# Splitting the positions around the second norm of the first block in a two-block kernel on one core

## The reference

```
merged = sigmoid(g_att) * y_att + sigmoid(g_conv) * y_conv
x = x + rms_norm(merged @ w_out, norm_mix_post)      # w_out 1024 x 1024
h = rms_norm(x, norm_ffn_pre)
u = causal_dwconv(h @ w_up, conv_ffn_w)              # w_up 1024 x 5632, three taps along the positions
a, g = split(u)
f = (gelu(g) * a) @ w_down                           # w_down 2816 x 1024
x = x + rms_norm(f, norm_ffn_post)
```

## Time and profile before

| | |
|---|---|
| median of 3 runs | 902.0 us (901.87 to 902.0) |
| the profiled execution, span from first to last instruction | 900.7 us |
| TensorE matmuls busy | 888.3 us |
| VectorE, ScalarE, GpSimd busy | 571.0, 496.2, 136.0 us |
| granted TensorE clock | 1.00 (2.4 GHz) over the span |
| share of TensorE in the chain that ended last | 83% |

### The profile page before, as it was taken

The page is one execution under the profiler, slowest core; times in us unless marked ns, Lnnn a source line. Parts: engine busy times, 40 slices in busy tenths (PEclk is TensorE's granted clock), DMA queues, the critical chain, the costliest instruction groups (busy, mean ns, idle before and its releaser), DMA issues.

```text
span 900.7 us, 15634 instructions
## 1 busy us (share of the span) xinstructions
PE 888.3 (99%) x6451; PEld 821.5 (91%) x6451; DVE 571.0 (63%) x824; ACT 496.2 (55%) x771; POOL 136.0 (15%) x151
## 2 busy tenths in 40 slices
PE   8999999999999999999999999999999999999998
PEld 8999999889999988788899988999999899998886
DVE  4556554878888746666767797765467655554542
ACT  5576864556656634566776764423454565554330
POOL 6011101611111100133443110000100011110000
PEclk9999999999999999999999999999999999999999
DMA  7843364665665566346544546542345656656560
GB/s 279 275 155 118 95 227 150 232 207 181 199 199 179 188 210 214 131 169 242 182 141 144 160 133 177 155 135 77 115 140 191 187 168 202 193 187 204 181 200 23
DMA packets 132594, 156.33 MB, mean 174 GB/s; under 512 B 9353, under 2 KB 106028, under 8 KB 132268
## 3 DMA queue, kind: packets, MB, share of 16 engines
q1 hardware_dynamic: 125844, 151.78, 51.9%
q10 hardware_dynamic: 6680, 3.56, 1.3%
HBM read 153.08 MB, written 2.24 MB: 172 GB/s over the span
## 4 chain that ended last, share of the span: by engine, by line
PE 83%; DVE 8%; DMA 3%; ACT 3%; issue 1%; POOL 1%; SPq 0%; ACTq 0%; POOLq 0%
PE ps L1979 72%; PE ps L1934 4%; PE ps L2010 3%; DVE wl L828 2%; PE ps L1931 2%; PE ps L2235 2%; DVE gv L862 1%; DVE gkq L862 1%; DMA U<-blocks 1%; DMA raw<-in_w_in 1%; DMA blocks<-last 1%; DVE mt L1267 1%; DMA Yc<-inverses 1%; ACT wh L1426 1%; DMA inverses<-Y 0%
## 5 line engine op out<-in xcount | busy, mean ns | idle before, releaser
L828 DVE TENSOR_TENSOR wl<-raw,wh 128x1024 fp32r<-128x1024 f32 (+1 forms) x275 | 326.4, 1205 | 190.0 <-ACT wh L1426 189.9
L1979 PE MATMUL ps<-xh,wh 128*128 128x256 f32 x1280 | 357.3, 282 | 0.7 <-ACT xh L1474 0.7
L1979 PE MATMUL ps<-xh,wl 128*128 128x256 f32 x1280 | 350.6, 277 | 0.0
L1426 ACT ACTIVATE wh<-raw 128x1024 fp32r<-128x1024 f32 (+1 forms) x292 | 286.6, 1024 | 115.4 <-PE ps L1979 93.0
L1979 PE MATMUL ps<-xl,wh 128*128 128x256 f32 x1280 | 348.3, 277 | 0.0
L1979 PEld LDWEIGHTS ps<-xh,wh 128*128 128x128 f32 x1280 | 238.9, 188 | 4.5 <-issue 1.4
L1979 PEld LDWEIGHTS ps<-xh,wl 128*128 128x128 f32 x1280 | 238.8, 188 | 0.0
L1979 PEld LDWEIGHTS ps<-xl,wh 128*128 128x128 f32 x1280 | 238.0, 188 | 0.3
L669 POOL TENSOR_TENSOR wl<-raw,wh 128x1024 fp32r<-128x1024 f32 (+1 forms) x17 | 44.2, 2600 | 81.6 <-ACT wh L1426 81.3
L1979 PE MATMUL ps<-wh,f2L 128*128 128x512 f32 x128 | 49.8, 389 | 0.0
L1979 PE MATMUL ps<-wl,f2H 128*128 128x512 f32 x128 | 49.8, 389 | 0.0
(11 more groups left out here) (334 smaller groups left out, 1363.8 us busy)
## 6 DMA issues: line engine op xcount, KB each, us to landing
raw<-in_w_in SPq DMA_DIRECT2D x55, 1024.0 KB, 5.1
raw<-in_w_up SPq DMA_DIRECT2D x38, 1024.0 KB, 5.2
raw<-in_w_down SPq DMA_DIRECT2D x26, 1024.0 KB, 5.0
raw<-in_w_out SPq DMA_DIRECT2D x8, 1024.0 KB, 5.1
raw<-in_w_proj_fox SPq DMA_DIRECT2D x4, 1024.0 KB, 5.1
raw<-in_w_proj_gdn SPq DMA_DIRECT2D x4, 1024.0 KB, 5.1
raw<-in_w_conv_branch SPq DMA_DIRECT2D x4, 512.0 KB, 3.4
raw<-in_w_att_branch SPq DMA_DIRECT2D x4, 512.0 KB, 3.3
```

The costliest lines, as they stand in the source:

```text
L828: e.tensor_tensor(L, R, H.bitcast(F32), ALU.subtract).then_inc(lo.sem)
L1426: e.activation(tile_of(WH, u)[:, k:kc, :], tile_of(RAW, u)[:, k:kc, :], ACT.Copy).then_inc(hi.sem)
L1979: k = e.matmul(o, l, r, start=opens, stop=done and n == ends[c], skip_group_check=True)
```

## The change

The last two output projection units (30, 31) are run by `part` first for positions 0 to 127 and then for 128 to 255, and so are the first two up units (32, 33) by a new `first_up`, which takes them with the activations stationary (as mode A does, 256 columns), into banks 7 and 3. The second norm is done for one half at a time by the functions that the second block's input already used, now with an index n. What units 32 and 33 give has positions on partitions; ScalarE copies it to XS (`keep_first_up`) and TensorE turns it back into the banks the convolution reads (`first_up_turn`). Their convolutions start in unit 34. The warm-up matmuls ahead of this norm and in it are gone. Unit 33 takes the fourth buffer pair. The low second half of unit 33, which VectorE made beside unit 31's `post`, is made with the first half, and both of unit 33's high halves stand ahead of ScalarE's `post` of unit 31. GpSimd does for each half both factors. The sync engine loads the gains of the norm (now applied from a row GN instead of a column) ahead of unit 33's weights, and spreads the loads that waited for the residual. The small weights are converted behind unit 40 instead of 32.

The diff, cut:

```diff
-WARM = (12, 4, 12)
+WARM = 12
-LATE_LO = frozenset([33])
...
+        AHEAD1, BEHIND1 = range(U_UP - 2, U_UP), range(U_UP, U_UP + 2)
+        AHEAD2, BEHIND2 = range(U_FQ - 3, U_FQ), range(U_FQ, U_FQ + 3)
+        SPARE = (BEHIND1[1], BEHIND2[0])
+        home, behind = {}, {}
+        for u in range(NU):
+            home[u] = NW if u in SPARE else (u - sum(s < u for s in SPARE)) % NW
+            behind[u] = max((v for v in range(u) if home[v] == home[u]), default=None)
...
+        FIRST_UP = (PS[7], PS[3])
... (sync)
-            for u in range(NRAW, U_UP + 3):
+            for u in range(NRAW, U_UP + 1):
+                weights(u)
+            e.wait_ge(*ymd("m", 3))
+            e.dma_start(GN[:], norm_ffn_pre[0].partition_broadcast(P)).then_inc(ld_gn, 16)
+            for u in range(U_UP + 1, U_UP + 5):
                 weights(u)
             e.wait_ge(*px("x", 1))
             e.dma_start(GP[:], norm_ffn_post[0].partition_broadcast(P)).then_inc(ld_gp, 16)
+            e.wait_ge(*nsc("up", 3))
             e.dma_start(GN[:], norm_mix_g_2[0].partition_broadcast(P)).then_inc(ld_gn, 16)
+            for u in range(U_UP + 5, U_UP + 10):
+                weights(u)
+            e.wait_ge(*ended(BEHIND1[1]))
             e.dma_start(gsw[:, :, 0:16], ...
-            for u in range(U_UP + 3, NU):
+            for u in range(U_UP + 10, NU):
... (GpSimd)
-            rstd(prs, 0, ss[:, 2:3], pred("sum", 0))
-            rstd(prs, 1, ss[:, 3:4], pred("sum", 1))
+            low(BEHIND1[0])
             for a in range(2):
+                rstd(prs, a, ss[:, 2 + a:3 + a], pred("sum", a))
                 e.wait_ge(*px("x", a))
                 rstd(nrs, a, ss[:, a:a + 1], nsq("sq", 2 + a))
... (VectorE, behind unit 29 and its post)
+            part(BEHIND1[0])
+            part()
+            low(BEHIND1[1], 0)
+            low(BEHIND1[1], 1)
+            post(0, AHEAD1[1], 1, 0)
+            x2_scaled(1, 0)
+            post(0, AHEAD1[1], 1, 1, ends=False)
+            x2_low(1, 0, 0)
+            post_ends(0, 1)
+            x2_low(1, 0, 1)
+            low(U_UP + 2, 0)
+            x2_scaled(1, 1)
+            low(U_UP + 2, 1)
+            x2_low(1, 1, 0)
+            x2_low(1, 1, 1)
+            part()
+            part(U_UP + 3)
...
+            for v in range(2, FC1):
+                unit(U_UP + v, 4 if v == 2 else None, first_up)
... (ScalarE, behind unit 29 and its post)
+            part(BEHIND1[0])
+            part(BEHIND1[1])
+            post(0, AHEAD1[1], 1, 0)
+            e.wait_ge(*px("x", 0))
+            squares(0)
+            high(U_UP + 2, 0)
+            post(0, AHEAD1[1], 1, 1)
+            x2_high(1, 0, 0)
+            x2_high(1, 0, 1)
+            e.wait_ge(*px("x", 1))
+            squares(1)
+            high(U_UP + 2, 1)
+            x2_high(1, 1, 0)
+            x2_high(1, 1, 1)
...
+            keep_first_up(0)
+            part()
+            part(U_UP + 3)
+            keep_first_up(1)
...
+            def first_up():
+                e.wait_ge(*upt("t"))
+                conv_begins(0)
+                conv_begins(1)
... (TensorE)
+            def first_up(u, a, at=None, begins=None):
+                H, L = tile_of(WH, u), tile_of(WL, u)
+                o = FIRST_UP[a][:, 256 * (u - U_UP):256 * (u - U_UP) + 256]
+                order = [(q, j) for q in range(8) for j in (0, 2)] + [(q, 1) for q in range(8)]
...
+                    k = e.matmul(o, (XH, XL, XH)[j][:, q, a * P:(a + 1) * P], (H, H, L)[j][:, q, :], start=n == 0, stop=n == 23,
...
+            def first_up_turn(a):
+                e.wait_ge(*upk("k", a))
+                for j in range(2):
...
+                    for c in range(2):
+                        k = turn(main_ps(U_UP + j)[:, c * 256 + a * P:c * 256 + (a + 1) * P],
+                                 XS[:, a, j * 256 + c * P:j * 256 + (c + 1) * P])
+                if a:
+                    k.then_inc(upt.sem)
+                    settle(7)
...
-            warm(WARM[0])
-            norm(1)
-            for v in range(FC1):
-                unit(U_UP + v, XH, XL, **(x_of(1) if v == 0 else {}))
-                if v == 0:
-                    settle(7)
+            for a in range(2):
+                for u in AHEAD1:
+                    part(u, a, m1H, m1L, lambda a, q: ymh("hi", q // 2), lambda a, q: ymd("lo", q // 2))
+            x2_turn(1, 0, 0)
+            x2_turn(1, 0, 1)
+            first_up(BEHIND1[0], 0)
+            first_up(BEHIND1[1], 0, at=3, begins=lambda: x2_turn(1, 1, 0))
+            x2_turn(1, 1, 1)
+            first_up(BEHIND1[0], 1)
+            first_up(BEHIND1[1], 1, at=2, begins=lambda: first_up_turn(0))
+            for v in range(2, FC1):
+                unit(U_UP + v, XH, XL, at=2 if v == 2 else None, begins=lambda: first_up_turn(1))
```

More of the change, by code:

```diff
@@ L1271, in vector, with first_convs @@
                     y_att_low(i)
-            def first_post(i):
-                if i:
-                    low(U_UP + 1, 1)
-                post(0, U_WO + 2 * i + 1, i, 0)
-            for i in range(2):
-                u = U_WO + 2 * i + 1
-                unit(u - 1)
-                unit(u, 5, lambda i=i: first_post(i))
-                post(0, u, i, 1)
-            scaled(1, 0)
-            scaled(1, 1)
-            norm(1, CG["ffn"])
-            soon.add(small_weights_low())
-            for v in range(FC1):
-                unit(U_UP + v)
+            u = U_WO + 1
+            unit(u - 1)
+            unit(u, 5, lambda: post(0, u, 0, 0))
+            post(0, u, 0, 1)
+            part(BEHIND1[0])
[15 more added lines that the diff above has]
+            part(U_UP + 3)
+            def first_convs():
+                yield from up_conv(0, 1)
+                yield from up_conv(1, 1)
+            def first_up():
+                soon.add(first_convs())
+            for v in range(2, FC1):
+                unit(U_UP + v, 4 if v == 2 else None, first_up)
                 soon.add(up_conv(v))
+                if v == 8:
+                    soon.add(small_weights_low())
+                if v == 2:
+                    soon.add(f_low(0))
                 if v % 2:
@@ L1421, in high @@
                     e.wait_ge(raw[s], 16 * (u // NRAW + 1))
-                    if u >= NW and u != U_FQ:
-                        e.wait_ge(*ended(u - NW - int(u in FIRST_X2)))
+                    if behind[u] is not None:
+                        e.wait_ge(*ended(behind[u]))
+                    elif u == SPARE[0]:
+                        e.wait_ge(*ymd("lo", 3))
                 elif u == 0:
@@ L1782, in scalar, with keep_first_up, conv_begins @@
                     y_att_high(i)
-            for i in range(2):
-                u = U_WO + 2 * i + 1
-                unit(u - 1)
-                unit(u, 5, lambda u=u, i=i: post(0, u, i, 0))
-                post(0, u, i, 1)
-            for a in range(2):
-                e.wait_ge(*px("x", a))
-                squares(a)
-            norm(1, CG["ffn"])
-            soon.add(small_weights_high())
-            for v in range(FC1):
-                unit(U_UP + v)
+            u = U_WO + 1
+            unit(u - 1)
+            unit(u, 5, lambda: post(0, u, 0, 0))
+            post(0, u, 0, 1)
+            part(BEHIND1[0])
[12 more added lines that the diff above has]
+            x2_high(1, 1, 1)
+            def keep_first_up(a):
+                end_of(BEHIND1[1], a)
+                copy(XS[:, a, 0:512], FIRST_UP[a][:]).then_inc(upk.sem)
+            keep_first_up(0)
+            part()
+            part(U_UP + 3)
+            keep_first_up(1)
+            def conv_begins(v):
                 i = v // 2
                 dst, cbase = (ya, yg)[v % 2][i % 2], (CG["cfa"], CG["cfg"])[v % 2] + 2 * FC1 + 2 * i
-                end_of(U_UP + v)
                 if i >= 2:
@@ L1804, in scalar, with first_up @@
                     soon.add(up_gelu(i))
+            def first_up():
+                e.wait_ge(*upt("t"))
+                conv_begins(0)
+                conv_begins(1)
+            for v in range(2, FC1):
+                unit(U_UP + v, 4 if v == 2 else None, first_up)
+                end_of(U_UP + v)
+                conv_begins(v)
+                if v == 8:
+                    soon.add(small_weights_high())
             def keep_fqk(n):
@@ L2028, in norm @@
                 for a in range(2):
-                    if a and n:
-                        warm(WARM[1])
                     for c in range(8):
@@ L2304, in tensor @@
             e.wait_ge(*cst("id"))
-            warm(WARM[2])
+            warm(WARM)
             e.wait_ge(ld_r, 16)
```

129 lines of the change are left out of this document (76 added, 53 removed).

## The result

The changed kernel takes 905.97 us in the median of 20 executions (902.38 to 908.91), the kernel before 902.46 in 20 (901.50 to 903.53): a ratio of 1.0036, interval 1.0026 to 1.0046. It is slower, by 3.3 us if that ratio is taken of 902.46, by 3.5 us by the medians. I had said 901.1, a range of 899.3 to 902.9, and gave slower 7%.

The account below looks back on a forecast made before the run. TensorE, busy 888.3 of 900.7 us, bounds the kernel; the prize is its 7.43 us stretch around the second norm. Unit 35 starts 0.9 us earlier: 900.7 - 0.9 + 1.3 = 901.1 us, range 899.3 to 902.9.

Parts of the forecast that it names:

- What stays the same: Output and up matmuls keep number, columns and times (0.227 and 0.113 us each); units 30 and 31 still end at 181.86.
- The clock: Rival, first up matmuls behind the new TensorE gap: half rate costs 2.7 to 5.5 us, 903.8 to 906.6; 6%.
- The chain of the first half: Second norm, first half: squares 177.7, reduction 179.3, xs 183.9, first up matmul 186.0; a 4.2 us gap replaces 7.43.
- The first rival: Norm hidden after all: squares at 176.42, up units at 183.9, 2.1 us earlier; 899.0, or up to 900.1; 17%.
- The wait for xl: First half of unit 32: xl's last four chunks ready at 188.65, wanted at 188.3, a 0.35 us TensorE wait.
- Second half hidden: Second half's norm in units 32 and 33: xs ready at 190.9 and 191.65, transposes due 191.15 and 192.3, no wait.
- turns on the path: Units 32 and 33 turned back by 8 TensorE transposes, 0.93 us, on the path; unit 33 ends at 198.65.
- The wait for taps: Unit 35 reuses unit 32's bank, whose taps VectorE finishes at 205.4: a TensorE wait of 0.4 us.
- The sum: Unit 35 begins at 205.4 instead of 206.3, gain 0.9 us: 900.7 - 0.9 + 1.3 = 901.1 us.
- The backlog on VectorE: Both early convolutions queue on VectorE; main case: no more waits; rival: units 35 to 37 wait, 902.1 to 903.5, 12%.

Follow-up runs that it names:

- the version with the post work first: Changed kernel with the first half's output projection post work ahead of unit 33's high halves on ScalarE and low halves on VectorE, no warm-up matmuls: 901.14 us.
- the first version with full-row matmuls: Changed kernel with 12 warm-up matmuls in the gap and two 128-row identity matmuls in place of unit 34's 64-row settling matmul: 901.31 us.
- the first four experiments: Changed kernel again, 906.61 us; kernel before without warm-up matmuls, 903.68; changed kernel with 12 warm-up matmuls, 902.56, or settling matmul at unit 34's end, 904.20.
- the two versions with the low half later: Post-work-first kernel with VectorE's second low half of unit 33 moved behind xl's second part: 904.16 us with the settling matmul, 900.87 us without.

## Why the prediction was wrong

- **What stays the same: wrong, and the step that failed.** "24 matmuls take 2.73 us", 96 x 0.1135 and 5.45 us a unit took the spacing of the kernel before for a constant of the instruction. It has two values here. Over units 35 to 53 the other one cost 4.05 us in the profiled execution, and 20 of 32 executions are high by about as much. "Nothing behind it changes: the chain stays on TensorE for 150 us" was the sentence that it broke. No rival had this mechanism. The trace of before held it: the up units are narrow in it, but the first units of the kernel, from 10 to 22 us, are wide.
- **The clock: wrong in its chance, too high in its price.** This is the second step that failed: the sum has it at nothing. I gave it 6% and 2.7 to 5.5 us. It fell in 27 of 32 executions and cost 1.4 us (with and without warm-up matmuls, both without the settling one). It alone would have put the forecast wrong: the eight executions of the first twenty that are not high all had a lower clock, and their median of 903.6 lies above my range too. That the 905.97 falls into this rival's 903.8 to 906.6 is luck; most of it is spacing. What I read as evidence against it, the idle 1.73 us that left the clock alone, did not stand for an idle 2.9 us; in the kernel before without warm-up matmuls, idle for 4.4 us, the clock falls in 12 of 12, and 0.72 us in the version with the post work first leaves it alone. The rule of the Trainium skill (TensorE: Matmul & The Clock Gate, Part 1), which I had set beside the row, was the better guide: by it an idle stretch closes the gate, and the traces agree, with 0.58 and 0.50 as granted clock from 186 to 190 us, at the end of the two gaps and behind them. I should have asked what the warm-up matmuls were for and put a price on losing it.
- **The chain of the first half: right.** High halves at 175.65 (I said 175.7), squares 177.57 (177.7), reduction 179.56 (179.3; the overlap with GpSimd cost 0.5, not 0.2), xs 184.14 (183.9), first up matmul 186.38 (186.0). The first rival's condition was then made in an experiment (the post work first) and gave its number: 184.12 against the 183.9 that I had worked out.
- **The wait for xl: not there.** xl's second part was ready at 188.77, near the 188.65 that I had; at the wide spacing TensorE asks for it only at 188.8.
- **Second half hidden, turns on the path: right.** The turns of xs run without a wait; the end of unit 33 is at 199.2 (198.65), late by 0.4 from the first up matmul and by 96 x 0.0045 = 0.43 from the spacing in units 32 and 33, and early by the 0.35 of the xl wait.
- **The wait for taps: the step was right, the wait was not there.** The taps are done at 205.70 (205.4). I had TensorE at unit 35 at 205.0, to wait 0.4 us; it came at 205.87, 0.17 us too late to wait. Behind every such wait in the profiles the spacing is narrow.
- **The sum.** 0.46 us won at unit 35 instead of 0.9. Unit 34 took 6.67 us where I had 6.33: its last 36 matmuls at the wide spacing are 0.16 of that, and the rest stands at the turns and the settling matmul, where the stream restarts. With the clock at 1.000 and the narrow spacing, the first version with full-row matmuls comes near the forecast, 901.31 against 901.1; it is another kernel, and the agreement within 0.2 us is in part luck. The clock adds 1.4, the spacing 4.05 in 20 of 32: 901.3 + 1.4 + 4.05 = 906.8, which is where the high executions lie (905.42 to 909.03).
- **The backlog on VectorE: right that it does not stay.** No wait behind unit 35 in any profile.

## What to carry to other kernels

Where a matmul-bound kernel moves by a few microseconds and no wait explains it, measure the spacing of back-to-back matmuls over the long stretches before and after; 4.4 ns over 914 matmuls, 4 us, is more than all the reordering here won. Take more than one execution for it: one profile shows one draw. Before you take warm-up matmuls out of a gap, ask whether the gap goes with them: they were worth 1.4 us here as long as it stayed, and with a gap of 0.7 us the clock held without them. When a chain is split by halves to be hidden, put the first half's work first in every queue; here the preparation of unit 33 ahead of it took 2.3 of the 5.4 us of cover (first up matmul at 186.38 instead of 184.12).

## What the runs showed of the hardware

Back-to-back matmuls of 256 columns with a 128-column weight load each run at one of two steady spacings, 113.3 or 117.8 ns, at the same granted clock of 1.00, with the same instructions. In the long stretches either lasts until something breaks the stream. The changed kernel's 12 first matmuls of unit 34, just behind its wide up halves, were narrow; the turns behind them then led to either, with the same instructions ahead (with the 64-row matmul behind the turns three profiles wide and four narrow, without it there three and four). Behind a wait at unit 35 the stream was narrow in nine of nine profiles. What in the engine differs stays open, and so does why the 64-row matmul does no such harm in the kernel before (3 of the 35 executions beside the first four experiments were at 906 or more, and none of the 122 others), and how much of its harm in the changed kernel is the wait that it takes away. A matmul of the kind takes the same 0.28 us in its record at either spacing, so only the starts tell.

A GpSimd operation on 128x1 elements took 1.41 us instead of 0.55 while VectorE made low halves beside it (the two versions with the low half later).
